# The order of VectorE's work in the gate steps of a two-block transformer kernel, with the high parts of H cast two tiles ahead

## The reference

```python
def chunk(args):
    xi, ei, gi = args
    hid = jax.nn.gelu(jnp.einsum("td,tkd->tk", xi, u_tab[ei]))
    return jnp.einsum("tk,tkd->td", gi * hid, v_tab[ei])
```

## Time and profile before

| | |
|---|---|
| median of 3 runs | 4147.49 us (4143.0 to 4148.52) |
| the profiled execution's own time | 4134.96 us |
| its span | 4133.2 us, 77923 instructions |
| TensorE matmul busy | 3633.6 us, 88% |
| DVE busy | 2505.4 us, 61% |
| ScalarE busy | 1392.3 us, 34% |
| mean granted TensorE clock | 0.93 |

### The profile page before, as it was taken

How to read it: one execution, slowest core, us unless ns; L and a number is a source line. 1 busy time by engine, 2 the same in 40 slices (tenths; PEclk the granted TensorE clock), 3 DMA queues, 4 the chain that set the end, 5 groups by cost and what they waited for, 6 DMA issues and landing times.

```text
span 4133.2 us, 77923 instructions
## 1 busy us (share of the span) xinstructions
PE 3633.6 (88%) x28720; PEld 3289.2 (80%) x28720; DVE 2505.4 (61%) x6350; ACT 1392.3 (34%) x2128; POOL 331.0 (8%) x216
## 2 busy tenths in 40 slices
PE   7779789899899887978998999988785999799898
PEld 6579789889899765978998989976554887587698
DVE  6359765766796553987566578746465223464544
ACT  3234224233233433332322423343242223332443
POOL 1237000000000012730000000000000000000000
PEclk9689899999999977989999999999897999899999
DMA  6534325334334554442433433331101222121153
GB/s 236 171 103 153 103 97 168 102 129 141 102 119 141 175 172 135 142 142 97 145 125 106 164 105 115 123 131 61 36 1 41 87 97 97 67 92 49 54 180 132
DMA packets 131691, 478.51 MB, mean 116 GB/s; under 512 B 14512, under 2 KB 16560, under 8 KB 130992
## 3 DMA queue, kind: packets, MB, share of 16 engines
q1 hardware_dynamic: 115696, 416.72, 30.0%
q0 software_dynamic: 15808, 59.25, 4.3%
HBM read 474.87 MB, written 1.05 MB: 115 GB/s over the span
## 4 chain that ended last, share of the span: by engine, by line
PE 72%; DVE 18%; issue 4%; ACT 3%; DMA 2%; DVEq 1%; POOL 0%; ACTq 0%; SPq 0%
PE bank L439 71%; DVE arena L1500 2%; ACT Wh L867 2%; DMA HA<-mods 1%; DVE Wl L1232 1%; DVE arena L1414 1%; DVE arena L1580 1%; DVE arena L1411 1%; DVE arena L1435 1%; DVE arena L1410 1%; DVE arena L1413 1%; DVE arena L1412 1%; PE bank L681 1%; DVE arena L1456 1%; DVE arena L1453 1%
## 5 line engine op out<-in xcount | busy, mean ns | idle before, releaser
L439 PE MATMUL bank<-HR,Wh 128*128 128x256 f32 (+1 forms) x12288 | 1864.7, 306 | 156.9 <-DVE HR L1575 60.0
L439 PEld LDWEIGHTS bank<-HR,Wh 128*128 128x128 f32 x12288 | 1681.1, 198 | 243.9 <-issue 77.2
L1232 DVE TENSOR_TENSOR Wl<-ring,Wh 128x1024 fp32r<-128x1024 f32 x692 | 847.3, 1225 | 1172.8 <-ACT Wh L867 1165.8
L867 ACT CAST Wh<-ring 128x1024 fp32r<-128x1024 f32 x788 | 823.5, 1045 | 836.9 <-PE bank L439 833.7
L439 PE MATMUL bank<-HR,Wl 128*128 128x256 f32 (+1 forms) x6144 | 951.8, 298 | 13.8 <-DVE Wl L1232 7.5
L439 PEld LDWEIGHTS bank<-HR,Wl 128*128 128x128 f32 x6144 | 848.1, 194 | 44.8 <-DVE Wl L1232 7.9
L439 PE MATMUL bank<-arena 128*128 128x32 bf16 (+4 forms) x6624 | 560.3, 256 | 135.9 <-issue 76.0
L439 PEld LDWEIGHTS bank<-arena 128*128 128x128 bf16 (+3 forms) x6624 | 442.0, 123 | 206.5 <-issue 151.8
L1028 ACT ACTIVATE arena<-bank 128x256 f32 x256 | 98.5, 385 | 788.8 <-PE bank L439 788.6
L1500 DVE TENSOR_SCALAR arena<-arena 128x128 bf16<-128x128 bf16 x2048 | 355.6, 251 | 0.1
L1726 POOL TENSOR_TENSOR Wl<-ring,Wh 128x1024 fp32r<-128x1024 f32 x96 | 247.5, 2591 | 146.2 <-ACT Wh L867 145.9
(11 more groups left out here) (222 smaller groups left out, 1938.9 us busy)
## 6 DMA issues: line engine op xcount, KB each, us to landing
ring<-weights SPq DMA_DIRECT2D x788, 512.0 KB, 3.3
HA<-mods POOLq DMA_DIRECT2D x96, 512.0 KB, 6.0
arena<-bias POOLq DMA_DIRECT2D x16, 256.0 KB, 2.9
arena<-keys POOLq DMA_DIRECT2D x2, 1024.0 KB, 5.6
HA<-mla POOLq DMA_DIRECT2D x1, 1536.0 KB, 6.7
K<-constants SPq DMA_DIRECT2D x1, 1402.0 KB, 5.8
X<-x SPq DMA_DIRECT2D x1, 1024.0 KB, 8.4
X<-context POOLq DMA_DIRECT2D x1, 1024.0 KB, 7.2
```

The costliest lines, as they stand in the source:

```text
L439: return nc.tensor.matmul(out, lhsT, rhs, start=first, stop=last)
L867: nc.scalar.copy(Wh[:, i % SPL], ring[:, i % RAW]).then_inc(S("hi_done"), 1)
L1232: v.tensor_tensor(Wl[:, i % SPL], ring[:, i % RAW], Wh[:, i % SPL], ALU.subtract).then_inc(S("lo_done"), 1)
```

## The change

`steps` can now write out the last pass too (`tail`), and `last(it)` tells that pass. In ScalarE's v phases H's high parts of tiles 0 and 1 are cast before the loop and step s casts that of tile s+2. In DVE's program H's low parts follow the same pattern (two before the loop, then s+2); in phases with gates the one-hots of step 0 are made before the loop, and step s does `gated(s-1)`, `spread(s+1)`, then the weight split of s+3. Nothing else is touched: TensorE's, GpSimd's and SP's programs stay as they are.

```diff
--- before.py
+++ after.py
@@ -225,12 +225,19 @@
         eng.wait_ge(sem, value)
 
 
-def steps(eng, n, peel, body):
+def steps(eng, n, peel, body, tail=False):
 
     if peel:
         body(0)
-    with eng.Fori(1 if peel else 0, n) as it:
+    with eng.Fori(1 if peel else 0, n - 1 if tail else n) as it:
         body(it)
+    if tail:
+        body(n - 1)
+
+
+def last(it):
+
+    return isinstance(it, int) and it == EQ // R - 1
 
 
 def build(nc, wts, mod_d, cst_d, keys_d, mla_d, bias_d, x_d, ctx_d, out_d, stop_after=None):
@@ -1003,18 +1010,23 @@
                     if kind == "v":
                         act.wait_ge(S("gm_ev"), NKEY * l + (q + 1) * EQ)
 
-                        def body(it, q=q, base=base):
+                        def h_high(s, it, q=q, base=base):
+
+                            act.wait_ge(S("tile_done"), base + s - MV + 1 + R * it)
+                            act.wait_ge(S("setup"), 1)
+                            nc.scalar.copy(Hh[:, s % MV, 0:T], GH[q % 2][:, bass.ds(it * R + s, 1), :]
+                                           .rearrange("p o t -> p (o t)")).then_inc(S("mv_hi"), 1)
+
+                        def body(it, base=base):
                             for s in range(R):
-                                n = NKEY * l + q * EQ + s + R * it
-
-                                act.wait_ge(S("tile_done"), base + s - MV + 1 + R * it)
-                                act.wait_ge(S("setup"), 1)
-                                nc.scalar.copy(Hh[:, s % MV, 0:T], GH[q % 2][:, bass.ds(it * R + s, 1), :]
-                                               .rearrange("p o t -> p (o t)")).then_inc(S("mv_hi"), 1)
+                                if s + 2 < R or not last(it):
+                                    h_high(s + 2, it)
                                 hi_next[0] = base + s + LEAD
                                 hi(base + s + LEAD, it)
 
-                        steps(act, EQ // R, False, body)
+                        for s in range(2):
+                            h_high(s, 0)
+                        steps(act, EQ // R, False, body, True)
                         hi_next[0] = base + EQ + LEAD
                         continue
                     if q >= 2:
@@ -1517,22 +1529,32 @@
                         v.tensor_tensor(g, g, bank[2 + s % 2][:, 0:BT * EQ].rearrange("p (t e) -> p e t", t=BT),
                                         ALU.mult).then_inc(S("gm_ev"), 1)
 
-                    def body(it, kind=kind, q=q, qb=qb, base=base):
+                    def h_low(s, it, q=q):
+
+                        dve.wait_ge(S("mv_hi"), NKEY * l + q * EQ + s + 1 + R * it)
+                        v.tensor_tensor(Hl[:, s % MV, 0:T], GH[q % 2][:, bass.ds(it * R + s, 1), :]
+                                        .rearrange("p o t -> p (o t)"), Hh[:, s % MV, 0:T], ALU.subtract)\
+                            .then_inc(S("mv_lo"), 1)
+
+                    def body(it, kind=kind, qb=qb, base=base):
                         for s in range(R):
-                            if kind == "v":
-                                dve.wait_ge(S("mv_hi"), NKEY * l + q * EQ + s + 1 + R * it)
-                                v.tensor_tensor(Hl[:, s % MV, 0:T], GH[q % 2][:, bass.ds(it * R + s, 1), :]
-                                                .rearrange("p o t -> p (o t)"), Hh[:, s % MV, 0:T], ALU.subtract)\
-                                    .then_inc(S("mv_lo"), 1)
+                            ahead = s + 1 < R or not last(it)
+                            if kind == "v" and (s + 2 < R or not last(it)):
+                                h_low(s + 2, it)
                             if qb is not None:
-                                spread(it, s)
+                                if s or not isinstance(it, int) or it:
+                                    gated(it, s - 1)
+                                if ahead:
+                                    spread(it, s + 1)
                             lo_next[0] = base + s + LEAD
                             lo(base + s + LEAD, it)
-                            if qb is not None and (s or not isinstance(it, int) or it):
-                                gated(it, s - 1)
-
-
-                    steps(dve, EQ // R, qb is not None, body)
+
+                    if kind == "v":
+                        for s in range(2):
+                            h_low(s, 0)
+                    if qb is not None:
+                        spread(0, 0)
+                    steps(dve, EQ // R, qb is not None, body, True)
                     if qb is not None:
                         gated(EQ // R - 1, R - 1)
                     lo_next[0] = base + EQ + LEAD
```

## The result

| | before | changed |
|---|---|---|
| median | 4145.27 us (4 runs, 4143.0 to 4148.52) | 3976.03 us (4 runs, 3967.63 to 3978.22) |
| ratio | | 0.9587, 95% interval 0.9571 to 0.9604 |
| profiled execution | 4134.96 us | 3978.22 us |

Forecast were 3981 and a range of 3955 to 4015. The kernel is 4.1% faster.

The account below looks back on a forecast made before the run. TensorE was taken as the bound (72% of the chain), losing time to waits and a lowered clock. Gains of 156 + 10 = 166 us off the 4147.5 median gave 3981 us, range 3955 to 4015.

Parts of the forecast that it names:

- part 1: U phases with gates: DVE's new order cuts the step to 4.37 us, phases to 142.9 (first 145.2), gaining 155.9.
- The ring: U step with gates: cast, split, gating, one-hots, product span two steps, 9.91 us, so 4.96 a step against TensorE's 4.37.
- the end of a phase: U phase with gates: 4.57 us from when the last product could start to the next tile, 4.90 less one gating.
- The clock: U phases with gates: about 34 us of the 155.9 gain comes from TensorE no longer dropping to 1.2 GHz behind waits.
- Rival C: Clock drops have another cause and stay, so the gain is 34 us smaller: 4015 us; chance 4%.
- part 2: V phase with gates: DVE's work rises to 4.12 of 4.37 us a step, TensorE still sets the step; cost 0.
- part 3: V phases without gates: H's parts cast two tiles ahead save 0.052 us on each of 192 tiles, 10 us.
- Rival B: V phases without gates: TensorE's own alternation makes 2.93 a tile, H's part gives nothing: 3991 us; chance 14%.
- part 4: Peeled last iterations: more code, possibly more instruction fetches; cost taken 0, bounds 0 and 12 us.
- A: U step with gates: a wait stays because DVE's in-order waits interleave otherwise, half the gain lost: 4059 us; chance 7%.
- D: Weight stream: loads wait for the later split, so weight tiles land late and it is slower: 4147 and above; chance 3%.
- E: U step with gates: the ring is closed by something misread, step and time stay: 4147 us; chance 2%.

Follow-up runs that it names:

- experiment 1: Changed kernel with DVE's new order alone, H's parts made in their own step and not ahead: 4004.44 us (4 runs), ratio 0.9665.
- experiment 3: Kernel before with one swap in DVE's gate step, gating s-1 moved in front of the split, nothing made ahead: 4101.96 us, one run.
- experiment 6: Changed kernel with H's parts made one tile ahead instead of two: 3972.30 us, one run.
- experiment 4: Changed kernel with three more products on DVE in each gate step, written to spare memory: 3995.10 us, one run.
- experiment 5: Changed kernel with six more products on DVE in each gate step, written to spare memory: 4138.65 us, one run.
- experiment 7: Changed kernel with a u phase's last split moved behind the last gating and H's first two low parts: 3962.74 us (5 runs), ratio 0.9548.
- experiment 2: Kernel before with H's parts made two tiles ahead, DVE's gate order left as it was: 4131.24 us (8 runs), ratio 0.9969.
- experiment 8: Kernel of experiment 7 without TensorE's wait for the copied gates: 3960.63 us (5 runs), ratio 0.9550.

## Why the prediction was right

**The u step with gates** (part 1). Right in mechanism and size: 142.4 to 142.9 for the second and third phases (142.9 forecast), 144.9 for the first (145.2), 158.0 us in all against 155.9. The ring is shown from three sides: taking it over three steps removed the wait, with H's part (the change) and without (experiment 1), and taking one member of 0.33 out of it shortened two steps by 0.33, from 10.01 to 9.68 in the loop and from 9.91 to 9.58 in front of it (experiment 3).

The term that I had too long is the end of a phase, 4.57, measured 4.15 to 4.23 at five of the six ends. These are ScalarE's first cast of H and DVE's first low part, in the kernel before and in the changed one:

```profile
621.86 0.41 ACT L1012 CAST HR<-arena 128x256 fp32r x1 [2.25 <-DVE arena L1517]
...
622.41 0.42 DVE L1524 TENSOR_TENSOR HR<-arena,HR 128x256 fp32r<-128x256 f32 x1 [0.87 <-ACT HR L1012]
```

```profile
593.84 1.01 ACT L1017 CAST HR<-arena 128x256 fp32r<-128x256 f32 x3 [1.62 <-DVE arena L1529]
594.27 1.17 DVE L1535 TENSOR_TENSOR HR<-arena,HR 128x256 fp32r<-128x256 f32 x3 [0.47 <-ACT HR L1017]
```

I took one gating of 0.33 off. The row for two gatings (0.74) goes down to one of 0.41 to 0.42, and ScalarE's first cast of H follows the gating's end by 0.04 instead of 0.33, now that it stands before ScalarE's loop and not in it; DVE's first low part, likewise in front of its loop, follows that cast's start by 0.43 instead of 0.55. With H's parts left in the loops this 0.4 is gone again: 142.82 against 142.40 (experiment 1). The sixth end, of the third u phase in the second layer, took 4.60: DVE's first low part started 0.88 after the cast there, and not 0.43 to 0.51. The later execution of the same kernel and experiment 6 have the same 0.88 at that place, experiments 4, 5 and 7 have 0.51. No run shows why.

**The clock.** I put it at 34 us. By the clock column, clock withheld in the six phases was 0.06 x 176.2 + 0.04 x 167.7 + 0.04 x 166.5 + 0.07 x 176.8 + 0.04 x 166.5 + 0.02 x 164.2 = 46 us before, and 0.02 x 144.9 x 2 = 6 after: 40, with rounding of some 5. The column also counts half clock in moments when TensorE idles, so this is more than the time lost. Counted by steps it is less: in the six phases of the kernel before, 21 of the short steps took 5.5 to 5.9 us instead of 4.4 to 4.6, some 29 us together (an estimate). Most of the remaining 5 of my 34 is no clock at all: I took two steps at 9.91, as in the first pass, for the whole phase, and in the loop they take 10.01 (experiment 3). The sum of the gain did not need this division. Rival C, that these drops have another cause and stay, is refuted: the clock is 1.00 in the second and third u phases of the changed kernel, and the first u and the v phase with gates are at half clock only within 7 us of their start. What the rows do not settle is which pause brings the clock down. It fell three or four times a phase over pauses of 1.03 in every second step (0.96). Over pauses of 0.5 in every step it did not fall in the third u phase of experiment 5 (1.00) and did in the second (0.97). The kernel before itself, in the third u phase of the second layer, had pauses of 0.82 and 0.28 in turn and kept its clock for 100 us:

```profile
2359.22:2460.00 100.78, 91.06 (x974) 87.47 (x973) 74.80 (x279) 27.04 (x42) 0.00 (x0) 1.00 0.31 105
```

In experiment 2 it fell over pauses of 0.80 and 0.81 (sixteen matmuls in 3.66 at 744.89). So I have no rule to give beyond this: with the pauses gone, so were the drops.

**The v phase with gates** (part 2). 0 forecast; 0.8 measured over both. DVE had 0.25 to spare by my sum, 0.22 by the loop's measured 4.15, and experiment 4 shows how little it is: 0.60 more and it is the limit. The sum hid something that only showed in experiment 1: with H made in its own step, the new order would have cost 2.5 and 3.1 us in these two phases. I had treated the two parts as independent; in this phase they are not.

**H ahead** (part 3). 10 forecast; 11.3 measured, of which 1.5 is one phase start that found the clock up (92.25 instead of 93.74), so 9.8 without that luck. Rival B falls with experiment 2. The two tiles are one more than needed (experiment 6).

**Written-out last passes** (part 4). 0 forecast, and in the u phases DVE still waits before splits only. The bound of 12 rested on a price of 1 us for each written-out pass that no row had shown. The profile's instruction queue q14 moved 0.61 MB in the changed kernel against 0.53 before, which fits the longer code; what that costs by itself was not measured, and the 0.37 us at the end with 4.60 may or may not belong to it. What the runs do show is that a written-out pass is the quicker one for DVE: 4.91 a step against 5.02 in the loop (experiment 5), which the changed kernel, paced by TensorE, can't use.

**Rivals A, D, E.** Inside the gate phases TensorE waits no more, except once in each layer at the start of the first u phase (experiment 8). ScalarE waits there for TensorE and for the last gating of a quarter, and never for a weight tile, so the later loads of D cost nothing.

**The level.** The sum was made against 4134.96 and moved up by 12.5 to the median shown. Profile against profile the change came out at 156.7, median against median at 169.2, phases against phases at 170.1; 166 was forecast. The phases are the measure to trust, since nothing outside them was changed. Of the 166, the two terms that were forecast as gains came out 2 and 1 above.

## What to carry to other kernels

When an engine works in order and one of its instructions waits for a late event (here the split for the cast of the tile just finished), write the ring of handovers from that event back to itself and count how many steps it spans; moving the instruction behind work that is made a step ahead adds a step to the ring and costs no work at all. Then compare the ring's length per step with each engine's sum of work: the larger is the new limit, and what is made ahead is a stock that a phase can use up once. Look at the first and last step of each loop on their own, since what stands first in line there decides how long the next phase waits.

## What the runs showed of the hardware that I had not expected

- ScalarE's first instruction inside a loop followed its release by 0.33 us (621.53 to 621.86 before; the same in experiment 1), the same instruction in front of the loop by 0.04 (593.80 to 593.84), at all six ends of either kernel. In the loop it also takes its address from the loop's counter; the runs don't separate the two.
- A gate step costs DVE 0.10 to 0.11 us more inside the loop than in a written-out pass: 5.02 against 4.91 in experiment 5, and 0.43 against 0.32 from the one comparison to the three products in the kernel before (788.03 to 788.47, 736.80 to 737.12).
- A row of three products lasts 0.70 us, but three more in line cost DVE 0.60 (1124.57 to 1125.17 in experiment 4): the row's last end overlaps the next instruction.
- The clock stayed up over some single pauses of 1.41 us behind 140 us of dense work (2.17 for sixteen matmuls at 595.25 in experiment 7) and fell after others; in the kernel before it fell within phases whose pauses of 1.03 recur every 10 us.
